# First expert unit of a hybrid encoder block: gather over four PSUM banks, expert order ahead of the weights, refills in smaller pieces

## The chip, the cores and the metric

One core of one Trainium2 chip runs the whole program. The metric is device time in microseconds (us); it is the slowest core's time, and here there is one core. All data are float32. The time of the kernel before is the median of three runs.

## The reference, cut to what matters

One encoder layer over 256 tokens of width 1024: RMS norm, projection, two attention groups, output projection and residual, then a two-level mixture of experts, then a final norm. The change lies where the attention part ends and the experts begin.

```python
def hier_moe(x, w_group, b_group, w_expert, b_expert, w_gate, w_up, w_down):
    xt = x.reshape(-1, d)                       # 256 tokens x 1024
    gl = xt @ w_group + b_group                 # 4 groups, top 1
    el = (xt @ w_expert + b_expert)             # 4 x 8 experts, top 2 in the group
    ...                                         # combine: weights of the two experts of a token
    for gi in range(4):                         # every expert: 1024x512, 1024x512, 512x1024
        h = silu(xt @ w_gate[gi]) * (xt @ w_up[gi])
        y = y + (h * combine[:, gi]) @ w_down[gi]
    return y
```

Each of the 32 experts has 3 matrices of 2 MiB, 201 MB in all, and every one is read from HBM once, whichever tokens chose it.

## The kernel before, in words

**Ring.** The weights of the experts pass through a ring of 12 slots of 2 MiB in SBUF. One matrix fills one slot: 16 KB in each of 128 partitions, which is 8 chunks of the contraction (KC = 8) of 2 KB each for gate and up. SP (SyncE) issues all weight DMAs on one queue, in a fixed order, and waits before each until the slot has been read.

**Units.** The 32 experts are worked off in ten units of 2 or 4 experts (WAYS = 2, 2, 4, 4, 2, 2, 4, 4, 4, 4). Units 0 and 1 are the fixed experts 0 to 3, so their 12 matrices are loaded during the attention part and fill the ring. From unit 2 on the experts are taken in order of how many tokens chose them. That order is known only after the router: it stands in `expert_at`, which VectorE (DVE) writes at L1096 with `order_ready`. SP reads the expert's number from there (`order_of`, L367 to L369, a register load for each expert) before it can issue the first load of unit 2.

**Refill of the first slots.** The two gate slots of unit 0 are refilled with the gate matrices of the first two experts of unit 2, in pieces (`GATE_PIECES`, `load_chunks`, L380 to L398): chunks 0 and 1, 2 and 3, then 4 to 7, each when TensorE (PE) has multiplied those chunks for both experts (`gate_pieces` at L1540, `gate_done`). The two up slots follow in halves (`load_piece`, L399 to L405, `up_half`), then down slots and unit 1's slots in halves. From unit 3 on whole slots are loaded (L435 to L440).

**Gather.** A unit's tokens are gathered by PE: a selection matrix `pick` (made by DVE, `make_picks`, L1028) is multiplied with the rows h, chunk by chunk and over the two token tiles. For unit 0 the first four chunks go to bank GD0 (`gather_tile`, L1543), tile 0 ahead of tile 1, so that PE can begin when `pick_first` is there; chunks 4 and 5 go to GD1, and chunks 6 and 7 to the same bank after the gate products of chunks 0 to 3. ScalarE (ACT, `gathered_out`, L705) takes chunks 0 to 3 out of PSUM, and signals each; DVE (L1048) takes the rest in two pieces (`xg_mid`, `xg_dve`). `first_gate` (L1530) multiplies a chunk once it is out.

**Order by hand on each engine.** PE, from the router's end: three constant products of 448 columns (`multiply_constants`, L1399, their results are not used), ranks of the first choices, one constant product, ranks of the second choices (`ranked`), four small products for the counts (`counted`), one constant product, `gather_tile`, `gather_chunks(1, 0..2)`, the product that turns the experts' places into an order (`ordered`, L1558), `first_gate` of 0..4, the gather of chunks 6 and 7, `first_gate` of the rest, then up. DVE, from `ranked` on: `rank1` (L1025), `make_picks`, the weights of the chosen experts (L1075 to L1080), `weigh_picks`, then counts, keys, places (L1084 to L1090), `wide_hot` (L1091), `place_hot` (L1093, `places_ready`), `expert_at`, `gathered_out(0)`.

Unit 1's gathers, transposes and unit 0's down products follow on PE (L1584 on). Its loop waits at L1601 until all early pieces of unit 2 have landed.

Of the kernel before, what the change touches and what calls it, by code (L numbers as in the profile page):

```python
# [10 lines left out]
ALU = mybir.AluOpType  # L11
# [23 lines left out]
GATE_PIECES = ((0, 2), (2, 4), (4, 8))  # L35
# [76 lines left out]
def fill_at(u, m, a):  # L112
    return 3 * sum(WAYS[:u]) + ways(u) * m + a
# [5 lines left out]
def build_encoder(nc, x, x_cols, norm1_g, w_in, qn_g, kn_g, sink, rel_bias, gnorm_a, gnorm_b, w_o, norm2_g,  # L119
# [11 lines left out]
    with ExitStack() as ctx:  # L131
# [131 lines left out]
        COUNTS, PICKS0, RANKS, ORDER = Y0, UP, Y2, Y3  # L263

# [24 lines left out]
        first_ready, second_ready, pick_first = map(sem, ("first_ready", "second_ready", "pick_first"))  # L289
# [25 lines left out]
        def _(sp):  # L315
# [83 lines left out]
            for k in range(2):  # L399
                if k == 0:  # L400
                    sp.wait_ge(up_half, 1)
                else:
                    sp.wait_ge(up_done, 1)
                load_piece(2, 0, 2, k, 2)
                load_piece(2, 0, 3, k, 2)  # L405
# [14 lines left out]
            for k in range(2):  # L420
                if k == 0:
                    sp.wait_ge(up_half, 2)
                else:
                    sp.wait_ge(up_done, 2)
                load_piece(2, 2, 0, k, 2, up_refill_in)
                load_piece(2, 2, 1, k, 2, up_refill_in)
# [144 lines left out]
        def _(act):  # L571
# [201 lines left out]
        def _(dve):  # L773
# [274 lines left out]
            def gathered_out(i):  # L1048
                if i == 0:
                    for k, done in enumerate((xg_mid, xg_dve)):  # L1050
                        dve.wait_ge(gathered, k + 2)
                        dve.tensor_tensor(xgT[:, 4 + 2 * k:6 + 2 * k, :], ps[GD1][:, 256 * k:256 * k + 256].rearrange("p (c s) -> p c s", c=2),
                                          bcast(g2_rows[:, 4 + 2 * k:6 + 2 * k], 2, P), ALU.mult).then_inc(done, 1)
                else:
                    dve.wait_ge(gathered, 2 * i + 3)
                    dve.tensor_tensor(xgT[:, 4:8, :], ps[GD1][:].rearrange("p (c s) -> p c s", c=4), bcast(g2_rows[:, 4:8], 2, P),  # L1056
                                      ALU.mult).then_inc(xg_dve, 1)
# [20 lines left out]
            k_second = mark(dve.tensor_tensor(w_second, hot2, bcast(w2, 3, PER_GROUP), ALU.mult))  # L1078
            after(k_second)
            link(dve.tensor_tensor(weight.rearrange("p t (g e) -> p t g e", g=GROUPS), w_first, w_second, ALU.add))  # L1080
# [8 lines left out]
            link(dve.tensor_reduce(place[0:EXPERTS], key_above[0:EXPERTS], AX_X, ALU.add))  # L1089
            link(dve.tensor_scalar(wide_e[0:EXPERTS], place[0:EXPERTS], float(WIDE), float(HALF_CAP), ALU.is_le, ALU.mult))  # L1090
            dve.tensor_tensor(wide_hot[0:EXPERTS], ident[0:EXPERTS, 0:EXPERTS],  # L1091
                              wide_e[0:EXPERTS].broadcast_to([EXPERTS, EXPERTS]), ALU.mult)
            dve.tensor_tensor(place_hot[0:EXPERTS], iota1[0:EXPERTS, 0:EXPERTS],  # L1093
                              place[0:EXPERTS].broadcast_to([EXPERTS, EXPERTS]), ALU.is_equal).then_inc(places_ready, 1)
            dve.wait_ge(ordered, 1)
            dve.tensor_copy(expert_at[:], ps[ORDER][0:1, 128:128 + EXPERTS]).then_inc(order_ready, 1)  # L1096
            gathered_out(0)
            make_picks(rank1, 2, 2)
# [86 lines left out]
        def _(pe):  # L1185
# [213 lines left out]
            def multiply_constants(n, bank):  # L1399
                for _ in range(n):  # L1400
                    pe.matmul(ps[bank][:, 0:448], ident, cst[:, 0:448], start=True, stop=True)
# [11 lines left out]
            multiply_constants(1, GATE)  # L1413
# [8 lines left out]
            multiply_constants(1, GATE)  # L1422
# [119 lines left out]

            def gather_tile(t, c):  # L1543
                return pe.matmul(ps[GD0][:, c * P:(c + 1) * P], h_cols[:, t, c, :], pick[:, t, :],
                                 start=(t == 0 and c == 0), stop=(t == TT - 1 and c == 3))
# [12 lines left out]
            pe.matmul(ps[ORDER][0:1, 128:128 + EXPERTS], expert_col, place_hot[0:EXPERTS], start=True, stop=True).then_inc(ordered, 1)  # L1558
# [6 lines left out]
            products(0, 2, fill_at(0, 1, 0), UP, up_done, up_half, KC // 2)  # L1565
# [18 lines left out]
            for i in range(1, UNITS):  # L1584
# [15 lines left out]
                if i == 2:  # L1600
                    pe.wait_ge(first_pieces_in, 16 * 2 * PIECES)  # L1601
# [125 lines left out]
```

## Time and profile before

| | |
|---|---|
| runs | 554.76, 555.28, 555.88 us, median 555.28 |
| profiled execution | span 553.0 us from the first to the last instruction; its own time is not listed apart from the runs, and the median is 2.3 us above the span |
| busy | PE 447.3 us (81%), PE weight loads 191.3, DVE 108.5, ACT 80.0, POOL 28.4 |
| DMA | 217.68 MB, mean 394 GB/s; the SP queue (q1) 214.84 MB, 93.5% of 16 engines' span |
| mean granted PE clock | 0.911 of 2.4 GHz |

A window row gives for a stretch of time the busy time of each engine with the number of its instructions, the granted PE clock as a share of full speed, the mean busy share of the 16 DMA engines and what they moved in GB/s. A timeline row gives start, duration, engine, line, operation, output and input, and how many instructions were merged. A "q" behind an engine means its instruction queue, as SPq for the DMA issues of SP.

### The profile page before, as it was taken

To read this page: it belongs to the slowest core of one execution; us is meant where nothing else is said; L and a number is where in the kernel's file an instruction comes from. 1 tells how busy PE (TensorE), PEld (TensorE's weight loads), DVE (VectorE), ACT (ScalarE), POOL (GpSimd) and SP (SyncE) were. 2 spreads that over 40 slices of the span, in tenths; PEclk is the share of its full clock that TensorE was granted. 3 is DMA by queue.
4 is the path that set the end of the run, shared out by engine and by line. 5 is a ranking of instruction groups with operands and counts; after the bars stand their busy time and mean duration, and the time that the engine had idled before them with its cause. 6 is when DMAs were issued, how large, how long until landed. Compare 5 with 4: busy or idle time off the path is not lost.

```text
span 553.0 us, 6311 instructions
## 1 busy us (share of the span) xinstructions
PE 447.3 (81%) x2496; PEld 191.3 (35%) x2496; DVE 108.5 (20%) x346; ACT 80.0 (14%) x212; POOL 28.4 (5%) x61
## 2 busy tenths in 40 slices
PE   8999999999999977569999984962784384666794
PEld 3455554664353332133442521410232021311231
DVE  1028863261140310020210400400031000400012
ACT  1127663221110101000101001000100001000103
POOL 0242422100000000000000000000000000000000
PEclk9999999999999999699999988876877887977999
DMA  8989995969999999999999999999999999999992
GB/s 314 352 320 422 395 339 180 373 247 364 424 420 423 427 429 424 429 427 430 425 428 430 422 430 425 430 425 429 429 425 430 425 428 428 427 428 430 420 387 105
DMA packets 26798, 217.68 MB, mean 394 GB/s; under 512 B 5224, under 2 KB 7016, under 8 KB 13200
## 3 DMA queue, kind: packets, MB, share of 16 engines
q1 hardware_dynamic: 22400, 214.84, 93.5%
q10 hardware_dynamic: 4368, 2.42, 1.5%
q8 instruction: 21, 0.34, 0.2%
q14 instruction: 9, 0.07, 0.0%
HBM read 216.18 MB, written 1.06 MB: 393 GB/s over the span
## 4 chain that ended last, share of the span: by engine, by line
PE 47%; DMA 44%; SPq 6%; issue 1%; DVE 1%; ACT 0%; POOLq 0%; POOL 0%; DVEq 0%; ACTq 0%
DMA ring<-in_w_down_dram 28%; PE bank L1466 11%; PE bank L1486 9%; DMA ring<-in_w_gate_dram 8%; PE bank L1201 7%; DMA ring<-in_w_up_dram 6%; PE bank L1289 5%; SPq L446 5%; PE bank L1427 2%; PE bank L1243 2%; PE bank L1267 1%; PE bank L1255 1%; PE bank L1520 1%; PE bank L1538 1%; PE bank L1528 1%; DMA ring<-in_w_in_dram 1%
## 5 line engine op out<-in xcount | busy, mean ns | idle before, releaser
L1466 PE MATMUL bank<-ring,head 128*32 128x512 f32 (+1 forms) x992 | 155.0, 676 | 69.7 <-DMA ring<-in_w_gate_dram 37.9
L1466 PEld LDWEIGHTS bank<-ring,head 128*32 128x32 f32 (+1 forms) x992 | 44.4, 128 | 170.9 <-issue 170.7
L1486 PE MATMUL bank<-ring,region_q 128*32 128x512 f32 (+1 forms) x512 | 79.5, 664 | 25.3 <-DMA ring<-in_w_down_dram 24.4
L1072 DVE COPY region_q<-bank 128x256 f32<-128x256 f32 x10 | 4.2, 424 | 301.8 <-PE bank L1445 301.8
L1486 PEld LDWEIGHTS bank<-ring,region_q 128*32 128x32 f32 (+1 forms) x512 | 23.0, 127 | 74.1 <-issue 70.4
L722 ACT ACTIVATE head<-bank 128x512 f32<-128x512 f32 x20 | 11.1, 595 | 243.2 <-PE bank L1520 229.6
L1201 PE MATMUL bank<-ring,head 128*128 128x512 f32 x96 | 43.1, 597 | 1.3 <-DMA ring<-in_w_in_dram 1.3
L1427 PEld LDWEIGHTS bank<-region_q,h 128*128 128x128 f32 x304 | 35.7, 192 | 9.1 <-issue 9.1
L1427 PE MATMUL bank<-region_q,h 128*128 128x128 f32 x304 | 38.5, 279 | 0.0
L1520 PE MATMUL bank<-head,region_q 128*128 128x512 f32 x72 | 33.3, 605 | 1.2 <-ACT head L722 1.2
L1289 PE MATMUL bank<-ring 128*128 128x512 f32 x64 | 29.7, 600 | 0.0
L708 ACT ACTIVATE head<-bank,head 128x128 f32<-128x128 f32 x40 | 11.4, 368 | 124.0 <-PE bank L1427 119.1
L1201 PEld LDWEIGHTS bank<-ring,head 128*128 128x128 f32 x96 | 17.5, 190 | 23.4 <-issue 22.5
L568 POOL TENSOR_TENSOR stat<-stat 128x1 f32<-128x1 f32 x2 | 1.1, 548 | 438.4 <-DVE stat L1168 438.4
L1520 PEld LDWEIGHTS bank<-head,region_q 128*128 128x128 f32 x72 | 12.9, 190 | 21.6 <-issue 19.6
L1289 PEld LDWEIGHTS bank<-ring 128*128 128x128 f32 x64 | 11.3, 190 | 10.8 <-issue 10.8
L1033 DVE TENSOR_SCALAR region_q<-cst,sorted_rw,stat 128x32 f32<-128x32 f32 (+1 forms) x56 | 12.4, 297 | 0.0
L1043 DVE TENSOR_SCALAR region_q<-cst,sorted_rw 128x32 f32<-128x32 f32 (+1 forms) x56 | 12.4, 297 | 0.0
L1066 DVE TENSOR_TENSOR region_q<-region_q,bank 128x512 f32<-128x512 f32 x10 | 6.9, 687 | 17.0 <-PE bank L1466 17.0
L1061 DVE COPY region_q<-bank 128x512 f32<-128x512 f32 x10 | 6.9, 692 | 16.0 <-PE bank L1480 16.0
L1056 DVE TENSOR_TENSOR head<-bank,head 128x512 f32<-128x512 f32 x9 | 6.2, 692 | 17.1 <-PE bank L1427 17.1
L855 DVE SCALAR_TENSOR_TENSOR h<-bank,stat,h 128x512 f32<-128x512 f32 x8 | 6.0, 751 | 16.4 <-PE bank L1289 9.8
(194 smaller groups left out, 290.9 us busy)
## 6 DMA issues: line engine op xcount, KB each, us to landing
ring<-in_w_gate_dram SPq DMA_DIRECT2D x28, 2048.0 KB, 39.4
ring<-in_w_up_dram SPq DMA_DIRECT2D x28, 2048.0 KB, 39.3
ring<-in_w_down_dram SPq DMA_DIRECT2D x24, 2048.0 KB, 38.1
ring<-in_w_down_dram SPq DMA_DIRECT2D x12, 1024.0 KB, 12.5
ring<-in_w_up_dram SPq DMA_DIRECT2D x8, 1024.0 KB, 10.6
ring<-in_w_gate_dram SPq DMA_DIRECT2D x6, 1024.0 KB, 9.4
ring<-in_w_o_dram SPq DMA_DIRECT2D x2, 2048.0 KB, 11.7
ring<-in_w_in_dram SPq DMA_DIRECT2D x7, 512.0 KB, 8.2
```

What stands on the lines that cost most here:

```text
L446: sp.dma_start(slots[fill_slot(fill_at(UNITS - 1, 2, a))][:, cols], down_e[bass.ds(experts[a], 1), :, cols].rearrange("a p d -> (a p) d")) ...
L708: last = act.activation(xgT[:, c, :], ps[GD0][:, c * P:(c + 1) * P], ACT.Copy, scale=g2_rows[:, c:c + 1])
L722: act.activation(y_slots[:, 512 * half:512 * half + 512], ps[(GD0 if i else Y0) + half][:], ACT.Copy).then_inc(y_ready, 1)
L1033: last = dve.tensor_scalar(pick[:, t, rows * a:rows * (a + 1)], iota1[:, 0:rows], ranks[:, t, e0 + a:e0 + a + 1], rstd2[:, t:t + 1], ALU.i ...
L1043: last = dve.tensor_scalar(pick_w[:, t, rows * a:rows * (a + 1)], iota1[:, 0:rows], ranks[:, t, e0 + a:e0 + a + 1], weights[:, t, e0 + a:e ...
L1201: return pe.matmul(ps[bank][:], xT[:, c, t * P:(t + 1) * P], cols, start=(c == 0), stop=(c == KC - 1))
L1243: last = pe.matmul(ps[2 * (s % 2) + half][:, 256 * j:256 * j + 256], qkT[rows, 5 * g + 2 * jg + j, qt * P:(qt + 1) * P], qkT[rows, 5 * g + ...
L1289: last = pe.matmul(ps[bank][:], mixT[:, 1 - g, t, c, :], w_o_sb[g][:, c, 512 * half:512 * half + 512], start=(c == 0), stop=(c == 3))
L1427: last = pe.matmul(ps[GD0 + b][:, c * P:(c + 1) * P], h_cols[:, t, 4 * b + c, :], pick[:, t, :], start=(t == 0), stop=(t == TT - 1))
L1466: last = pe.matmul(ps[bank][rows, :], xgT[:, c, rows], slots[fill_slot(f + a)][:, c * F:(c + 1) * F], start=(c == 0), stop=(c == KC - 1))
L1486: last = pe.matmul(ps[bank + half][rows, :], hT[:, c, rows], slots[fill_slot(f + a)][:, c * D + 512 * half:c * D + 512 * half + 512], star ...
L1520: last = pe.matmul(ps[Y0 + k][:], place_w[i % 2][:, (k // 2) * P:(k // 2 + 1) * P], y_slots[:, 512 * (k % 2):512 * (k % 2) + 512], start=( ...
```

## The change

Six edits, all around unit 0:

1. The gate refill of unit 2's first two experts goes in four pieces of two chunks instead of three pieces, the refill of the two up slots in quarters instead of halves (`up_half` now counts three times for unit 0).
2. The gather of unit 0 is written in four steps of two chunks (both token tiles), each into a bank of its own (GD0, Y1, GD1, Y2). The first two come first, the other two after the gate products of chunks 0 to 3. `pick_first` is gone: the gather waits for all of `pick`.
3. ACT waits for the first two chunks, then for the next two. DVE waits for steps 3 and 4.
4. On DVE the counts' keys, the places and `place_hot` come straight after `make_picks`; the weights, `wide_hot`, `counts` and `weigh_picks` come later.
5. PE makes the order's product right after the first two gather steps.
6. The constant product between the two ranks is 128 columns wide instead of 448; the one behind the counts is gone.

```diff
-GATE_PIECES = ((0, 2), (2, 4), (4, 8))
+GATE_PIECES = ((0, 2), (2, 4), (4, 6), (6, 8))
+        FIRST_BANKS = (GD0, Y1, GD1, Y2)
...
@@ SP
-            for k in range(2):
-                if k == 0:
-                    sp.wait_ge(up_half, 1)
+            for k in range(4):
+                if k < 3:
+                    sp.wait_ge(up_half, k + 1)
                 else:
                     sp.wait_ge(up_done, 1)
-                load_piece(2, 0, 2, k, 2)
-                load_piece(2, 0, 3, k, 2)
+                load_piece(2, 0, 2, k, 4)
+                load_piece(2, 0, 3, k, 4)
...
-                    sp.wait_ge(up_half, 2)
+                    sp.wait_ge(up_half, 4)
@@ ACT
-                act.wait_ge(gathered, 2 * i + (2 if i else 1))
+                if i:
+                    act.wait_ge(gathered, 2 * i + 3)
                 for c in range(4):
-                    last = act.activation(xgT[:, c, :], ps[GD0][:, c * P:(c + 1) * P], ACT.Copy, scale=g2_rows[:, c:c + 1])
+                    if i == 0 and c % 2 == 0:
+                        act.wait_ge(gathered, c // 2 + 1)
+                    last = act.activation(xgT[:, c, :], ps[GD0 if i else FIRST_BANKS[c // 2]][:, c * P:(c + 1) * P], ACT.Copy, scale=g2_rows[:, c:c + 1])
@@ DVE
-            make_picks(rank1, 0, 2, (pick_first, pick_ready))
-            k_w = mark(dve.tensor_tensor(w2, w1, e2, ALU.mult))
-            k_first = mark(dve.tensor_tensor(w_first, hot1_here, bcast(w1, 3, PER_GROUP), ALU.mult))
-            after(k_w)
-            k_second = ...
-            after(k_second)
-            link(... weight ...)
-            weigh_picks(rank1, weight, 0, 2)
-
+            make_picks(rank1, 0, 2, (None, pick_ready))
             dve.wait_ge(counted, 1)
-            dve.tensor_copy(counts, ps[COUNTS][:, 0:32])
             dve.tensor_tensor(key_row ...)
             link(... key_col ...)
             link(... key_above ...)
             link(dve.tensor_reduce(place ...))
+            dve.tensor_tensor(place_hot ...).then_inc(places_ready, 1)
+            k_w = ...
+            k_first = ...
+            dve.wait_ge(ordered, 1)
+            dve.tensor_copy(expert_at[:], ps[ORDER][0:1, 128:128 + EXPERTS]).then_inc(order_ready, 1)
             link(... wide_e ...)
-            dve.tensor_tensor(wide_hot ...)
-            dve.tensor_tensor(place_hot ...).then_inc(places_ready, 1)
-            dve.wait_ge(ordered, 1)
-            dve.tensor_copy(expert_at ...).then_inc(order_ready, 1)
+            dve.tensor_tensor(wide_hot ...).then_inc(order_ready, 1)
+            dve.tensor_copy(counts, ps[COUNTS][:, 0:32])
+            after(k_w)
+            k_second = ...
+            after(k_second)
+            link(... weight ...)
             gathered_out(0)
+            weigh_picks(rank1, weight, 0, 2)
@@ PE
-            multiply_constants(1, GATE)
+            multiply_constants(1, GATE, P)
...
-            multiply_constants(1, GATE)
...
-                    if c in (1, 3, KC - 1):
+                    if c in (1, 3, 5, KC - 1):
...
-            pe.wait_ge(pick_first, 1)
-            for c in range(4):
-                gather_tile(0, c)
+            def first_gather(k):
+                for c in (2 * k, 2 * k + 1):
+                    for t in range(TT):
+                        last = pe.matmul(ps[FIRST_BANKS[k]][:, c % 4 * P:(c % 4 + 1) * P], h_cols[:, t, c, :], pick[:, t, :],
+                                         start=(t == 0), stop=(t == TT - 1))
+                last.then_inc(gathered, 1)
+
             pe.wait_ge(pick_ready, 1)
-            for c in range(4):
-                last = gather_tile(1, c)
-            last.then_inc(gathered, 1)
-            gather_chunks(1, range(0, 2)).then_inc(gathered, 1)
-            for a in range(2):
-                landed(fill_at(0, 0, a))
-            pe.wait_ge(places_ready, 1)
-            pe.matmul(ps[ORDER] ...).then_inc(ordered, 1)
-            first_gate(range(0, 4))
-            pe.wait_ge(xg_mid, 1)
-            gather_chunks(1, range(2, 4)).then_inc(gathered, 1)
+            first_gather(0)
+            first_gather(1)
+            pe.wait_ge(places_ready, 1)
+            pe.matmul(ps[ORDER] ...).then_inc(ordered, 1)
+            for a in range(2):
+                landed(fill_at(0, 0, a))
+            first_gate(range(0, 4))
+            first_gather(2)
+            first_gather(3)
+            pe.wait_ge(xg_mid, 1)
             first_gate(range(4, 6))
             pe.wait_ge(xg_dve, 1)
             first_gate(range(6, KC))
-            products(0, 2, fill_at(0, 1, 0), UP, up_done, up_half, KC // 2)
+            products(0, 2, fill_at(0, 1, 0), UP, up_done, up_half)
...
-                pe.wait_ge(order_ready, 1)
+                pe.wait_ge(order_ready, 2)
...
-                    pe.wait_ge(first_pieces_in, 16 * 2 * PIECES)
+                    pe.wait_ge(first_pieces_in, 16 * 2 * (PIECES + 2))
```

## Rows read from the trace of the kernel before

**Rows 1.** The page, part 2: GB/s in 40 equal slices of 13.8 us.

```profile
GB/s 314 352 320 422 395 339 180 373 247 364 424 420 423 427 429 424 429 427 430 425 428 430 422 430 425 430 425 429 429 425 430 425 428 428 427 428 430 420 387 105
```

**Rows 2.** The chain that ended last: shares by engine, and its last wait.

```profile
PE 47%; DMA 44%; SPq 6%; issue 1%; DVE 1%; ACT 0%; POOLq 0%; POOL 0%; DVEq 0%; ACTq 0%
...
522.20 17.91 DMA ring<-in_w_down_dram
```

**Rows 3.** Windows: us, five engines' busy times, clock, DMA share, GB/s.

```profile
117.40:121.20 3.80, 3.78 (x26) 2.22 (x26) 1.77 (x12) 2.42 (x5) 0.00 (x0) 1.00 0.03 6
121.20:122.20 1.00, 1.00 (x8) 0.29 (x4) 0.00 (x0) 0.00 (x0) 0.00 (x0) 1.00 0.00 0
122.20:129.50 7.30, 7.30 (x40) 3.00 (x38) 1.32 (x5) 0.60 (x1) 0.00 (x0) 1.00 0.90 277
129.50:141.26 11.76, 11.76 (x70) 5.91 (x68) 1.38 (x2) 1.14 (x4) 0.00 (x0) 1.00 1.00 405
141.26:181.90 40.64, 39.77 (x239) 17.04 (x236) 9.17 (x33) 3.52 (x8) 0.00 (x0) 1.00 1.01 422
181.90:500.00 318.10, 229.83 (x1418) 89.17 (x1417) 37.25 (x124) 19.01 (x49) 0.00 (x0) 0.86 1.01 428
```

**Rows 4.** What SP's DMA queue waited for, 117 to 129 us.

```profile
SPq L369 <- DVE expert_at L1096: 12.7, 1, 12.7
```

**Rows 5.** Timeline and line view of SP's DMA issues.

```profile
121.22 0.36 SPq L384 DMA_DIRECT2D ring<-in_w_gate_dram  x1
...
122.35 1.42 SPq L384 DMA_DIRECT2D ring<-in_w_gate_dram  x3
...
127.61 0.34 SPq L384 DMA_DIRECT2D ring<-in_w_gate_dram  x1
...
141.26 4.24 SPq L376 DMA_DIRECT2D ring<-in_w_up_dram  x4
...
L340 SPq DMA_DIRECT2D ring<-in_w_gate_dram x4: 332/332/342, 181.9 to 183.5; - x4
```

**Rows 6.** Timeline of PE, DVE and ACT, 113 to 124 us.

```profile
113.28 1.00 PE L1401 MATMUL bank<-cst 128*128 128x448 f32 x2
...
114.78 0.22 DVE L1025 SCALAR_TENSOR_TENSOR rank<-bank,region_q 128x64 f32<-128x64 f32 x1
...
115.03 0.98 DVE L1033 TENSOR_SCALAR region_q<-cst,rank,stat 128x64 f32<-128x64 f32 x4
...
115.23 1.02 PE L1401 MATMUL bank<-cst 128*128 128x448 f32 x2
...
116.09 1.95 PE L1544 MATMUL bank<-region_q,h 128*128 128x128 f32 x16
...
117.66 0.17 DVE L1085 TENSOR_TENSOR region_q<-bank,cst 32x32 f32<-32x32 f32 x1
...
118.08 1.14 ACT L708 ACTIVATE head<-bank,head 128x128 f32<-128x128 f32 x4 [4.86 <-PE bank L1544]
...
118.34 0.14 DVE L1090 TENSOR_SCALAR region_q<-region_q 32x1 f32<-32x1 f32 x1
...
118.63 0.17 DVE L1093 TENSOR_TENSOR stat<-cst,region_q 32x32 f32<-32x32 f32 x1
...
118.95 0.21 PE L1558 MATMUL bank<-stat,cst 32*1 32x32 f32 x2
119.09 3.65 PE L1538 MATMUL bank<-ring,head 128*64 128x512 f32 x16
119.20 0.18 DVE L1096 CAST expert_at<-bank 1x32 int32<-1x32 f32 x1 [0.40 <-PE bank L1558]
...
122.67 1.16 PE L1427 MATMUL bank<-region_q,h 128*128 128x128 f32 x8
```

**Rows 7.** Windows as in rows 3: small packets, and a gap on PE.

```profile
128.00:129.00 1.00, 1.00 (x8) 0.32 (x6) 0.00 (x0) 0.06 (x1) 0.00 (x0) 1.00 1.03 410
531.00:535.00 4.00, 4.00 (x40) 2.77 (x36) 1.38 (x2) 1.19 (x2) 0.00 (x0) 1.00 1.02 399
166.50:167.70 1.20, 0.33 (x5) 0.17 (x5) 0.69 (x1) 0.00 (x0) 0.00 (x0) 1.00 1.03 430
```

More of the change, by code:

```diff
@@ L288, in build_encoder @@
         gexp_asked, e2_asked, chosen_ready, ranked, counted, flag_ready = map(sem, ("gexp_asked", "e2_asked", "chosen_ready", "ranked", "counted", "flag_ready"))
-        first_ready, second_ready, pick_first = map(sem, ("first_ready", "second_ready", "pick_first"))
+        first_ready, second_ready = map(sem, ("first_ready", "second_ready"))
         k_squared, ssk_ready, final_g_turned, final_g_cut = map(sem, ("k_squared", "ssk_ready", "final_g_turned", "final_g_cut"))
@@ L1050, in gathered_out @@
                     for k, done in enumerate((xg_mid, xg_dve)):
-                        dve.wait_ge(gathered, k + 2)
-                        dve.tensor_tensor(xgT[:, 4 + 2 * k:6 + 2 * k, :], ps[GD1][:, 256 * k:256 * k + 256].rearrange("p (c s) -> p c s", c=2),
+                        dve.wait_ge(gathered, k + 3)
+                        dve.tensor_tensor(xgT[:, 4 + 2 * k:6 + 2 * k, :], ps[FIRST_BANKS[2 + k]][:, 256 * k:256 * k + 256].rearrange("p (c s) -> p c s", c=2),
                                           bcast(g2_rows[:, 4 + 2 * k:6 + 2 * k], 2, P), ALU.mult).then_inc(done, 1)
                 else:
-                    dve.wait_ge(gathered, 2 * i + 3)
+                    dve.wait_ge(gathered, 2 * i + 4)
                     dve.tensor_tensor(xgT[:, 4:8, :], ps[GD1][:].rearrange("p (c s) -> p c s", c=4), bcast(g2_rows[:, 4:8], 2, P),
@@ L1089, in _ @@
             link(dve.tensor_reduce(place[0:EXPERTS], key_above[0:EXPERTS], AX_X, ALU.add))
+            dve.tensor_tensor(place_hot[0:EXPERTS], iota1[0:EXPERTS, 0:EXPERTS],
+                              place[0:EXPERTS].broadcast_to([EXPERTS, EXPERTS]), ALU.is_equal).then_inc(places_ready, 1)
+            k_w = mark(dve.tensor_tensor(w2, w1, e2, ALU.mult))
+            k_first = mark(dve.tensor_tensor(w_first, hot1_here, bcast(w1, 3, PER_GROUP), ALU.mult))
+            dve.wait_ge(ordered, 1)
+            dve.tensor_copy(expert_at[:], ps[ORDER][0:1, 128:128 + EXPERTS]).then_inc(order_ready, 1)
             link(dve.tensor_scalar(wide_e[0:EXPERTS], place[0:EXPERTS], float(WIDE), float(HALF_CAP), ALU.is_le, ALU.mult))
             dve.tensor_tensor(wide_hot[0:EXPERTS], ident[0:EXPERTS, 0:EXPERTS],
-                              wide_e[0:EXPERTS].broadcast_to([EXPERTS, EXPERTS]), ALU.mult)
-            dve.tensor_tensor(place_hot[0:EXPERTS], iota1[0:EXPERTS, 0:EXPERTS],
-                              place[0:EXPERTS].broadcast_to([EXPERTS, EXPERTS]), ALU.is_equal).then_inc(places_ready, 1)
-            dve.wait_ge(ordered, 1)
-            dve.tensor_copy(expert_at[:], ps[ORDER][0:1, 128:128 + EXPERTS]).then_inc(order_ready, 1)
+                              wide_e[0:EXPERTS].broadcast_to([EXPERTS, EXPERTS]), ALU.mult).then_inc(order_ready, 1)
+            dve.tensor_copy(counts, ps[COUNTS][:, 0:32])
+            after(k_w)
+            k_second = mark(dve.tensor_tensor(w_second, hot2, bcast(w2, 3, PER_GROUP), ALU.mult))
+            after(k_second)
+            link(dve.tensor_tensor(weight.rearrange("p t (g e) -> p t g e", g=GROUPS), w_first, w_second, ALU.add))
             gathered_out(0)
+            weigh_picks(rank1, weight, 0, 2)
             make_picks(rank1, 2, 2)
@@ L1397, in _, with multiply_constants @@
             router_logits(1, range(4, 8)).then_inc(routed, 1)
-            def multiply_constants(n, bank):
+            def multiply_constants(n, bank, cols=448):
                 for _ in range(n):
-                    pe.matmul(ps[bank][:, 0:448], ident, cst[:, 0:448], start=True, stop=True)
+                    pe.matmul(ps[bank][:, 0:cols], ident, cst[:, 0:cols], start=True, stop=True)
             def rank_tiles(hot, start):
@@ L1539, in first_gate @@
                                          start=(c == 0), stop=(c == KC - 1))
-                    if c in (1, 3, KC - 1):
+                    if c in (1, 3, 5, KC - 1):
                         last.then_inc(gate_done if c == KC - 1 else gate_pieces, 1)
-            def gather_tile(t, c):
-                return pe.matmul(ps[GD0][:, c * P:(c + 1) * P], h_cols[:, t, c, :], pick[:, t, :],
-                                 start=(t == 0 and c == 0), stop=(t == TT - 1 and c == 3))
-            pe.wait_ge(pick_first, 1)
-            for c in range(4):
-                gather_tile(0, c)
+            def first_gather(k):
[4 more added lines that the diff above has]
+                last.then_inc(gathered, 1)
             pe.wait_ge(pick_ready, 1)
-            for c in range(4):
-                last = gather_tile(1, c)
-            last.then_inc(gathered, 1)
-            gather_chunks(1, range(0, 2)).then_inc(gathered, 1)
+            first_gather(0)
+            first_gather(1)
+            pe.wait_ge(places_ready, 1)
+            pe.matmul(ps[ORDER][0:1, 128:128 + EXPERTS], expert_col, place_hot[0:EXPERTS], start=True, stop=True).then_inc(ordered, 1)
             for a in range(2):
                 landed(fill_at(0, 0, a))
-            pe.wait_ge(places_ready, 1)
-            pe.matmul(ps[ORDER][0:1, 128:128 + EXPERTS], expert_col, place_hot[0:EXPERTS], start=True, stop=True).then_inc(ordered, 1)
             first_gate(range(0, 4))
+            first_gather(2)
+            first_gather(3)
             pe.wait_ge(xg_mid, 1)
-            gather_chunks(1, range(2, 4)).then_inc(gathered, 1)
             first_gate(range(4, 6))
```

2 lines of the change are left out of this document (removed).

## The prediction, made blind

> **What bounds the kernel now.** I read the slices of the page first. GB/s stands at 420 to 430 from the eleventh slice to the last but two, and in the seventh to tenth it is 180, 373, 247 and 364 [rows 1]. So this is a kernel that streams 217 MB, and it loses time where the stream stops. The chain that ended last says the same: DMA 44%, and PE 47% in the part before the stream takes over. Its last wait is a DMA of a down matrix from 522.20 for 17.91 us, and from there a tail of 12.9 us runs to the end of the span at 553.0 [rows 2]. The windows show where the stream stops: from 117.40 to 121.20 nothing but a remnant moves (6 GB/s), from 122.20 to 129.50 it comes up at 277, then 405, then 422 up to 181.90 and 428 from there to 500 [rows 3]. From 181.90 on the engine busy shares do not matter. Every microsecond by which the stream starts earlier after 117.4 moves the end by as much, if the stream does not stop again.
>
> Who starts it? SP's queue waited 12.7 us for `expert_at` [rows 4]. The order was written at 119.20 + 0.18 = 119.38, but the first issue is at 121.22, the second at 122.35 (a register load for the next expert lies between) and two more follow within 1.42 us [rows 5]. The first gate products run from 119.09 for 3.65 us, four chunks [rows 6], so chunks 0 and 1 are done about 1.8 to 1.9 us after their start, at 121.0. The later of SP's two conditions is thus PE having read the slots, not the order. A stream that starts earlier needs the gate products earlier.
>
> **The change part by part.**
>
> *Constant product between the ranks, 448 to 128 columns.* Two passes take 1.00 us from 113.28 [rows 6]; the second choices are ready in their midst. 320 columns less in each pass, at 1.00 us for two passes of 448 with their fixed parts, can free at most 0.5 us of PE. But the four rank products behind keep their own load-and-multiply chain, and DVE reaches `rank1` only after its own weights' arithmetic. `rank1` starts at 114.78 [rows 6]. Bounds are 0 and 0.2 us; I take 0.13.
>
> *The constant product behind the counts goes.* It takes 1.02 us from 115.23, and the gather starts at 116.09 behind it [rows 6]. The new gather waits for all of `pick`. The picks run from 115.03 to 116.01; with 0.13 off, 115.88, plus about 0.25 us from DVE's signal to PE's first product (weights must be loaded first): 116.13. So the gather starts where it did, and the constants' 1.02 us is worth nothing here: it was hidden behind the picks. In exchange PE stands for some 0.7 us. In a like gap, 166.50 to 167.70 with PE busy 0.33, the granted clock stayed 1.00 [rows 7]. I cost it at nothing; if the clock fell to 1.2 GHz, the gather and gate products would stretch, and this step with them.
>
> *Gather in four steps.* 16 instructions take 1.95 us and the 8 of chunks 4 and 5 another 0.9, up to 118.9; only then come the order's product (118.95) and the first gate product (119.09) [rows 6]. Now steps 0 and 1 are 16 instructions and step 2 and 3 come later: the order's product can run at 116.13 + 1.95 = 118.08 and the gate products at 118.10, if their inputs are there. ACT needs 1.14 us for four chunks [rows 6], some 0.37 for the first one, and now starts on chunk 0 after half of the gather, at 117.2; it has chunk 0 at 117.6, chunk 3 at 118.8. No stall. Gate products start 1.0 us earlier.
>
> *Order ahead of weights.* From the first key at 117.66 to `place_hot` at 118.63 + 0.17 are 1.14 us, and `wide_e` at 118.34 shows where `place_hot` can now stand: 0.29 earlier [rows 6]. Right behind the picks that gives 115.85 + 0.68 + 0.17 = 116.7, two microseconds before 118.8. PE is not there to use it until 118.1, so the order is written at about 118.35, 1.0 us earlier. SP needs less than the 1.13 us between its first two issues to turn it into an address [rows 5], so it is ready by 119.5 and then waits for the gate chunks, as now. The weights and `weigh_picks` come later on DVE; they are first needed by unit 1, more than 10 us on, so nothing waits.
>
> *First refill.* Chunks 0 and 1 are read 1.0 us earlier: 118.10 + 1.9 = 120.0; issue at 120.2 instead of 121.22. The second expert's load stays 1.13 us behind it, pieces 3 and 4 come at 121.9 and 122.4. **Gain of the stream's start: 1.0 us** (bounds 0.3, if ACT or the places are late, and 1.2).
>
> *PE afterwards.* Steps 2 and 3 (16 instructions, about 2.0 us) take the place of one piece of 8 in 1.16 us at 122.67 [rows 6]. So PE gives back 0.85 of its 1.0 us: gate ends about 0.1 us earlier than now, and so do up and all that follows. `xg_mid` comes one multiply on DVE after step 2; step 3 (0.9 us) covers it.
>
> *Finer refills.* Twelve issues of 512 KB take the place of six of 1 MB, at about 0.43 us of SP each, every 1.7 us or so: SP has time. They come earlier only for chunks 4 and 5 (about 125.7 instead of 127.61) and quarters 1 and 3. Is the stream short of work there now? From 122.20 to 141.26 it moved 277 x 7.30 + 405 x 11.76 = 6.8 MB, and four matrices, 8.4 MB, had been issued: 1.6 MB, 3.8 us, were still queued at the 141.26 issue [rows 3, 5]. The same sum at 181.90 gives 23.9 of 25.2 MB, 2.9 us queued; less the 1.0 us from the issue at 121.22 to the first bytes after 122.20 [rows 3, 5], 1.9 us of slack. Two things follow: earlier issues find the queue full already, so they gain little; and a stream moved ahead by 1.0 us against PE's 0.1 does not run dry at either place, but nothing over 2.0 us could be gained in this way.
>
> What do they cost? Packets halve to 4 KB. The nearest rows: 410 GB/s in 128 to 129, when 4 KB pieces alone move from a filled queue; 399 in 531 to 535, with 4 and 2 KB packets [rows 7]; and 277 in the opening [rows 3]. The same 6.3 MB moved at about 405 in 8 KB packets, 15.5 us. At 410 they cost nothing or bring 0.2 us, at 399 they cost 0.25, at 277 they would take 22.7 us, 7.2 more. The queue is filled, so I stay near 399 and take **0.3 us lost**.
>
> **Sum.** 1.0 - 0.3 = 0.7 us off the span of 553.0, so 552.3, and with the 2.3 us that lie around the profiled span to the median of the runs, 554.6. That is 0.13% of 555.28; a measurement of this kernel tells about 0.2%, 1.1 us, from no change.
>
> **The rivals.**
>
> *A, small pieces starve the stream (slower).* Place: 128 to 144 us, the twelve pieces. The opening shows what 512 KB pieces do when each meets a short queue: 2.0 MB in 7.3 us [rows 3]. Whatever first bytes cost would be paid twelve times. It decides below 6.3 MB in 16.5 us, 381 GB/s: there the 1.0 us is gone. At 350 the stretch takes 18.0 us and the kernel 555.28 + 2.5 - 1.0 = 556.8; at 277 it would be 561.5. Against it: 3.8 us are queued. The Trainium skill, DMA: Bandwidth & Descriptors, section Bandwidth, has the rule "Batch DMAs to ≥1 MiB for ≥75% of peak", with 341 GB/s for a single 1 MB; by that figure, an estimate, the stretch would take 18.4 us and the kernel come to 557.2. The trace speaks against the rule for a queue with work in it, with 410 GB/s in 512 KB pieces. Chance 0.12.
>
> *B, the finer pieces feed the opening (larger gain).* The opening lost 7.3 - 2.0/0.423 = 2.5 us and the stretch behind it another 0.5. If that comes of few packets in flight, pieces 5 and 6, now 2 us earlier, and the quarters win back about 1 us. Up to the cap of 2.0: 553.3. For it: 405 against 422 with the queue not dry. Against it: the slow part is pieces 1 to 3, whose spacing the change leaves alone. Chance 0.25.
>
> *C, the start does not move.* One of the inputs is late (ACT's chunks, or the gather behind `pick_ready` instead of `pick_first`), and the first issue stays at about 121: 555.5 with the small packets' price. Chance 0.10.
>
> **How the numbers follow.** Forecast 0.53, A 0.12, B 0.25, C 0.10. The likeliest is 554.6, its own range 553.9 to 555.3 by the bounds of start and packets. Half a microsecond more for the scatter of the runs (554.76 to 555.88) puts some 0.1 of the forecast's chance over the 1.1 us mark; with most of B that is 0.34 faster. Same is the rest of the forecast with C and the near part of A, 0.54; slower 0.12. The range, 553.2 to 556.6, takes in B, C and A down to 355 GB/s.
>
> **What the profile after would show.** Right: the order written at 118.3 to 118.5, the first gate product at 118.1, the first gate refill issued at 120.1 to 120.4, gate products ending within 0.2 us of 127.4, no slow window between 129 and 182, the last down transfer landing 0.5 to 1 us earlier. Wrong start: an issue after 120.6. Wrong packets: under 395 GB/s from 130 to 144. Wrong cap: a window under 400 GB/s behind 141 or 182. A PE clock of 0.5 near 116 would overthrow the PE part.

## The result and the profile after

The changed kernel came out slower: 556.18 us median of 19 runs against 555.18 of the kernel before, ratio 1.0027, 95% interval 1.0016 to 1.0037, so 1.5 us (0.9 to 2.1) by the ratio; the two medians differ by 1.0. The forecast was 0.7 us faster. In a later comparison (e11 below) the same kernel stood at 0.9998 (0.9979 to 1.0017). Why one kernel gives both is the subject of what follows, and part of it stays open.

The page of the changed kernel, its span, its slices and its chain:

```profile
span 554.0 us, 6326 instructions
...
PEclk9999999989999999689999998977978887977898
...
GB/s 313 350 323 426 388 337 188 366 247 353 419 421 421 425 428 429 426 429 430 421 431 427 428 425 429 426 429 428 426 431 426 425 429 427 428 427 431 418 385 99
...
PE 47%; DMA 43%; SPq 7%; DVE 1%; issue 1%; ACT 0%; POOLq 0%; POOL 0%; DVEq 0%; ACTq 0%
```

Against [rows 1] the stream is no better where it was to gain: 247 in the ninth slice as before, 353 for 364 in the tenth. And PEclk has an 8 in the ninth slice, 111 to 125 us. Windows of the changed kernel (columns as in [rows 3]) show that place, and then the stretches of [rows 3]:

```profile
114.90:115.77 0.87, 0.00 (x1) 0.00 (x1) 0.87 (x6) 0.00 (x0) 0.00 (x0) 1.00 1.10 471
...
116.80:120.20 3.40, 3.40 (x16) 2.16 (x16) 0.88 (x6) 2.13 (x5) 0.00 (x0) 0.50 0.20 80
...
122.20:129.50 7.30, 7.30 (x44) 3.51 (x42) 2.63 (x10) 0.60 (x1) 0.00 (x0) 1.00 0.87 291
...
129.50:141.26 11.76, 11.76 (x70) 5.88 (x68) 1.38 (x2) 1.14 (x4) 0.00 (x0) 1.00 1.00 381
141.26:181.90 40.64, 39.76 (x236) 17.07 (x236) 9.17 (x33) 3.52 (x8) 0.00 (x0) 1.00 1.01 420
181.90:500.00 318.10, 229.16 (x1430) 89.38 (x1422) 37.33 (x124) 19.02 (x49) 0.00 (x0) 0.88 1.01 427
```

PE stood for 0.87 us behind the counts, and from 116.80 to 120.20 its granted clock was 0.50, the 1.2 GHz level. Behind that the stream moved at 381 where it had moved at 405. From 141 on the two kernels are alike. The timeline of the changed kernel shows what the half clock did:

```profile
110.45 0.26 DVE L970 SCALAR_TENSOR_TENSOR region_q<-bank,stat,router_b 128x36 f32<-128x36 f32 x1 [1.16 <-PE bank L1385]
...
114.47 0.22 DVE L1029 SCALAR_TENSOR_TENSOR rank<-bank,region_q 128x64 f32<-128x64 f32 x1
...
115.77 2.88 PE L1548 MATMUL bank<-region_q,h 128*128 128x128 f32 x16 [0.87 <-DVE region_q L1037]
...
116.32 0.18 DVE L1085 TENSOR_TENSOR stat<-cst,region_q 32x32 f32<-32x32 f32 x1
...
118.76 4.35 PE L1540 MATMUL bank<-ring,head 128*64 128x512 f32 x16
118.87 0.18 DVE L1090 CAST expert_at<-bank 1x32 int32<-1x32 f32 x1 [2.16 <-PE bank L1556]
...
121.59 2.55 SPq L385 DMA_DIRECT2D ring<-in_w_gate_dram  x4
```

The 16 gather instructions took 2.88 us for 1.95 in [rows 6], the 16 of the gate 4.35 for 3.65. `place_hot` (L1085) was there at 116.50 (forecast 116.7), two microseconds before PE could use it. But the order was written at 119.05, and the first refill issued at 121.59, not 120.2: 0.37 us later than before, where 1.0 us earlier was wanted.

**How the profiles are compared.** The attention part ahead of all this ends at another time in each execution: the router's last logits, the DVE row at 110.45 above, came between 109.7 and 112.4 us over all profiles. So each is read from its own such row, called R. The row of the kernel before, for R = 110.57:

```profile
110.57 0.25 DVE L966 SCALAR_TENSOR_TENSOR region_q<-bank,stat,router_b 128x36 f32<-128x36 f32 x1 [1.16 <-PE bank L1382]
```

The first issue then stands at R + 10.65 before and at R + 11.14 after. And the refill wave is measured by what the DMA engines moved from R + 9 to R + 36, a window of 27 us: 1 GB/s more or less there is 27/423 = 0.064 us of the stream that follows at 423. Six profiles of the changed order with small pieces and an undisturbed clock will give 337 to 343, so one profile is good to some 3 GB/s, 0.2 us. Windows of the kernel before and the changed one:

```profile
119.57:146.57 27.00, 27.00 (x144) 11.95 (x142) 3.53 (x9) 3.88 (x8) 0.00 (x0) 1.00 0.88 336
```

```profile
119.45:146.45 27.00, 27.00 (x145) 12.21 (x142) 4.34 (x14) 3.98 (x8) 0.00 (x0) 0.99 0.87 325
```

11 GB/s less, 0.7 us lost by R + 36. In the 40 us behind it the two move 423 and 421 GB/s, 0.2 us more, and that is no more than such windows scatter (421 to 423 over all kernels).

### The profile page after: what moved, and what is told of

It is laid out like the page before. It is cut to its first block, busy times and chain, and to the rows that moved or that the text cites. A ratio compares the mean times of both kernels' runs of the same rounds, so it can differ in the third digit from the quotient of the medians.

```text
span 554.0 us, 6326 instructions
## 1 busy us (share of the span) xinstructions
PE 446.0 (81%) x2494; PEld 191.4 (35%) x2494; DVE 108.4 (20%) x346; ACT 80.2 (14%) x212; POOL 28.7 (5%) x61
## 4 chain that ended last, share of the span: by engine, by line
PE 47%; DMA 43%; SPq 7%; DVE 1%; issue 1%; ACT 0%; POOLq 0%; POOL 0%; DVEq 0%; ACTq 0%
DMA ring<-in_w_down_dram 28%; PE bank L1468 11%; PE bank L1488 9%; DMA ring<-in_w_gate_dram 8%; PE bank L1204 7%; DMA ring<-in_w_up_dram 6%; SPq L447 6%; PE bank L1292 5%; PE bank L1429 2%; PE bank L1246 2%; PE bank L1270 1%; PE bank L1258 1%; PE bank L1540 1%; PE bank L1522 1%; PE bank L1530 1%; DMA ring<-in_w_in_dram 1%
## 5 line engine op out<-in xcount | busy, mean ns | idle before, releaser
L726 ACT ACTIVATE head<-bank 128x512 f32<-128x512 f32 x20 | 11.1, 595 | 240.4 <-PE bank L1522 225.7
L1429 PEld LDWEIGHTS bank<-region_q,h 128*128 128x128 f32 x288 | 33.7, 192 | 8.2 <-issue 8.2
L1429 PE MATMUL bank<-region_q,h 128*128 128x128 f32 x288 | 36.3, 279 | 0.0
```

Of the source, the lines that this page charges most:

```text
L726: act.activation(y_slots[:, 512 * half:512 * half + 512], ps[(GD0 if i else Y0) + half][:], ACT.Copy).then_inc(y_ready, 1)
L1429: last = pe.matmul(ps[GD0 + b][:, c * P:(c + 1) * P], h_cols[:, t, 4 * b + c, :], pick[:, t, :], start=(t == 0), stop=(t == TT - 1))
```

## The experiments

**First: are there two losses, and do they add?** Edits against the changed kernel (e1, e2, e3) and against the kernel before (e4).

e1, the constant product back behind the counts:

```diff
             pe.matmul(ps[COUNTS][0:EXPERTS, 32:33], chosen[:, 1, :], ones[:, 0:1], start=False, stop=True).then_inc(counted, 1)
+            multiply_constants(1, GATE)
```

> The changed kernel with the constant product of 448 columns behind the counts put back, nothing else. Clock theory (PE idle for 0.87 us behind the counts let the granted clock fall to 0.5 from 116.8 to 120.2, and that ate the earlier start): the clock stays at 1.00, the first gate product starts at 118.1, the first gate refill is issued at 120.2 instead of 121.6, and the time is 1.4 us below the changed kernel, 0.1 us above the kernel before. Packet theory alone (the twelve 512 KB pieces cost all of the loss): the time stays 1.5 us above the kernel before, though the first issue moves. Rival (the PE gap has nothing to do with the clock): the clock still falls at 116.8 and the issue stays at 121.6.

e2, the old piece sizes, no constant product:

```diff
-GATE_PIECES = ((0, 2), (2, 4), (4, 6), (6, 8))
+GATE_PIECES = ((0, 2), (2, 4), (4, 8))
...
-            for k in range(4):
+            for k in range(2):
...
-                load_piece(2, 0, 2, k, 4)
-                load_piece(2, 0, 3, k, 4)
+                load_piece(2, 0, 2, k, 2)
+                load_piece(2, 0, 3, k, 2)
```

with the semaphores' counts as before the change.

> The changed kernel with the refills in the old sizes (gate in three pieces, up in halves), nothing else; no constant product behind the counts, so the clock fall should stay. Packet theory: 129.5 to 144 moves at 405 GB/s or more instead of 381, mean landing of the last up piece 0.9 us earlier, time 0.9 us below the changed kernel, 0.6 above the kernel before. Clock theory alone: no difference to the changed kernel, 1.5 us above the kernel before.

e3, both edits:

> The changed kernel with both put back: the constant product behind the counts and the old piece sizes. What is left is the gather in four steps, the order ahead of the weights and the narrow product between the ranks. If the two losses add (1.4 and 0.9 us): 2.3 us below the changed kernel, 0.8 us below the kernel before, first issue at 120.2, clock 1.00 throughout. If something else in the new order costs time: no better than the kernel before.

e4, the kernel before with the pieces of the change, e2's edit the other way round:

> The kernel before with the finer refills alone (gate in four pieces, up in quarters). Packet theory: 0.9 us above the kernel before, with 381 GB/s in 129.5 to 141.3 against 405. If the finer pieces cost only where the clock fall delays PE: 0 to 0.2 us.

Measured against the kernel before on the same chip (interval in brackets; the row "changed" is from the first comparison):

| | first issue, us after R | GB/s, R+9 to R+36 | clock near the gather | ratio |
|---|---|---|---|---|
| before | 10.65 | 336 | 1.00 | |
| changed | 11.14 | 325 | 0.50 | 1.0027 (1.0016 to 1.0037) |
| e1 filler | 9.57 | 337 | 1.00 | 1.0002 (0.9984 to 1.0020) |
| e2 coarse | 9.57 | 349 | 1.00 | 1.0019 (0.9998 to 1.0039) |
| e3 both | 9.57 | 351 | 1.00 | 0.9996 (0.9975 to 1.0016) |
| e4 before, fine | 10.66 | 333 | 1.00 | 1.0006 (0.9988 to 1.0024) |

The windows of e1 to e4 in this order, each from its own kernel:

```profile
120.88:147.88 27.00, 27.00 (x148) 12.55 (x146) 4.70 (x13) 3.26 (x8) 0.00 (x0) 1.00 0.92 337
```

```profile
119.29:146.29 27.00, 27.00 (x148) 12.55 (x146) 4.70 (x13) 3.27 (x8) 0.00 (x0) 1.00 0.91 349
```

```profile
118.98:145.98 27.00, 27.00 (x148) 12.54 (x146) 4.70 (x13) 3.26 (x8) 0.00 (x0) 1.00 0.91 351
```

```profile
119.07:146.07 27.00, 27.00 (x144) 11.94 (x142) 3.53 (x9) 3.90 (x8) 0.00 (x0) 1.00 0.89 333
```

e1 and e3 had the first issue where the forecast had put it, 1.1 us earlier than before. Between e1 and e3 lie only the piece sizes: 14 GB/s, 0.9 us. In the kernel before the same pieces took 3 GB/s, 0.2 us, which is within the scatter of one profile. The times of whole runs are too wide to tell these four apart. e1's time was where clock theory had it. e3's was 0.2 us below the kernel before and not 0.8, with an interval that holds both. The surprise was e2: no constant product, the same gap on PE (0.86 us), and no fall of the clock. The clock theory as I had put it, gap means fall, had failed.

**Second: is the fall a matter of chance, and what else is to be gained?** e8 is e2 once more; e5 puts a constant product of 128 columns where e1 has 448; e6 has old piece sizes and takes out all constant products there. e7 is e3 with one edit on SP:

```diff
-            experts = order_of(2, range(1))
+            experts = order_of(2, range(2))
...
-                if k == 0:
-                    experts += order_of(2, range(1, 2))
```

> The kernel of e2 once more (changed kernel, old piece sizes, no constant product behind the counts). In e2's profile the clock had not fallen, in the changed kernel's it had, with the same work on PE up to there. Chance theory (with this gap the clock falls in some executions and not in others): either is possible; if it falls, the first issue stands at 11.1 us after the router's last logits instead of 9.6, and the last transfer of the first refill wave about 1.2 us later than in e2. Rival (the piece sizes decide over the clock): it does not fall here either. Time over all runs 0.5 to 1 us above the kernel before.

> The changed kernel with old piece sizes and a constant product of 128 columns behind the counts instead of 448: PE's gap shrinks from 0.87 to about 0.6 us. Chance theory: the clock falls less often than without it; in one profile either can show. If it stays, first issue at 9.6 us after the router's last logits; if it falls, at about 11.1.

> The changed kernel with old piece sizes and no constant products at all between the router and the gather (the three, the one between the ranks, the one behind the counts all gone): PE stands for most of the 5 us. Clock theory: the clock falls in every execution, and earlier; the first gate product and the first issue come 1.4 to 2.5 us later than in e3, relative to the router's last logits (issue at 11 to 12 us instead of 9.6). Rival (gaps do not matter to the clock here): issue at 9.6 or earlier, clock 1.00.

> The kernel of e3 (constant product behind the counts back, old piece sizes) with SP reading the numbers of both first experts before its first issue, where it waits for the gate chunks anyway; so the second expert's piece follows the first by 0.5 us instead of 1.13. Opening theory (the stream comes up slowly because its second piece comes late): mean landing of the fourth piece 0.5 us earlier after the router's last logits than in e3 (17.6 instead of 18.1 us), time 0.5 us below e3, about 1.3 us below the kernel before. Rival (the opening is slow by itself, whatever is queued): no difference to e3.

In e8 the clock fell, with the same code as e2. Its gap, its half clock and its refill wave (R = 111.44):

```profile
115.89:116.75 0.86, 0.00 (x1) 0.00 (x1) 0.86 (x6) 0.00 (x0) 0.00 (x0) 1.00 1.02 438
117.58:120.99 3.41, 3.41 (x17) 2.46 (x18) 0.99 (x7) 1.76 (x5) 0.00 (x0) 0.50 0.20 79
...
120.44:147.44 27.00, 27.00 (x145) 12.21 (x142) 4.51 (x16) 4.15 (x9) 0.00 (x0) 0.99 0.84 324
```

324 GB/s against e2's 349: **one fall of the clock costs 25 GB/s, 1.6 us, of one and the same kernel.** The first issue came at R + 11.13, as in the changed kernel and 1.56 us later than in e2, so the later start is the whole price. e8's ten runs lie between 551.96 and 557.47, four of them at or under 553.11 and six from 554.49 up; e8's ratio is 0.9992 (0.9971 to 1.0012). Two kinds of executions could look like that. But R alone scatters by 2.7 us over the profiles, and the runs without a profile show neither their R nor their clock there.

e5: a gap of 0.45 us, no fall, first issue at R + 9.58, 345 GB/s; one profile settles nothing. In e6 PE stood from 110.47 for 2.35 us, and the clock fell 2.1 us after the gap's start, before its end, and for twice as long:

```profile
110.47:112.82 2.35, 0.00 (x1) 0.00 (x0) 2.21 (x16) 0.21 (x1) 0.00 (x0) 0.94 1.03 439
112.60:119.40 6.80, 6.27 (x30) 6.12 (x31) 3.98 (x26) 0.83 (x3) 0.00 (x0) 0.50 0.73 312
```

First issue at R + 11.41, 315 GB/s in its refill wave.

e7 had the fourth piece landed at R + 17.44 against e3's 18.14 (mean of the 16 engines' landings). Over all undisturbed profiles of the new order the fourth piece landed at R + 17.76 to R + 18.42 with the number read between the pieces (ten profiles, mean 18.08), and at 17.44 to 17.72 with it read early (e7, e9, e12, mean 17.59): the opening did gain 0.5 us, as expected. But by R + 36 e7 stood where e3 stood, at 349 GB/s against 351. The hole is behind the fourth piece, for the next one is a whole half slot and waits for the end of the gate products:

```profile
128.00:130.00 2.00, 2.00 (x12) 0.70 (x10) 0.00 (x0) 0.00 (x0) 0.00 (x0) 1.00 0.90 229
```

e7's runs gave 0.9983 (0.9970 to 0.9997), the first kernel to beat the kernel before beyond its interval.

**Third: which of the finer pieces costs?** e9 is e7 and e10 is e3, each with the gate refill in four pieces as in the change and the up refill still in halves:

```diff
-GATE_PIECES = ((0, 2), (2, 4), (4, 8))
+GATE_PIECES = ((0, 2), (2, 4), (4, 6), (6, 8))
...
-                    if c in (1, 3, KC - 1):
+                    if c in (1, 3, 5, KC - 1):
```

> The kernel of e7 with the gate refill in four pieces as in the changed kernel, the up refill still in halves. In e7 the stream had a hole: 229 GB/s from 128 to 130, because the fourth piece was in before the next, whole-half piece could be issued. Feeding theory: the hole closes (over 350 GB/s there), the last up piece lands 0.9 to 1.4 us earlier after the router's last logits than in e7 (34.05), capped by what unit 2's last slots allow (1.2 us), time 0.9 us below e7, about 1.9 below the kernel before. Packet theory (every 512 KB piece costs by its size): no difference to e7 or 0.2 us worse.

> The kernel of e3 with the gate refill in four pieces, the up refill in halves, no early reading of the second number. With e1 (all fine) and e3 (all coarse) it tells which half of the finer refills costs. Feeding theory: p4 to last up piece 15.92 us in e3, 16.93 in e1; here 15.0 to 15.4, as the hole of e3 (315 GB/s from 128 to 130) closes and the up pieces stay large; time 0.6 us below e3. Packet theory: 16.3, halfway between e1 and e3, time 0.4 above e3.

e9 and e10, R + 9 to R + 36:

```profile
119.75:146.75 27.00, 27.00 (x148) 12.55 (x146) 4.70 (x13) 3.26 (x8) 0.00 (x0) 1.00 0.93 349
```

```profile
119.43:146.43 27.00, 27.00 (x148) 12.54 (x146) 4.70 (x13) 3.26 (x8) 0.00 (x0) 1.00 0.92 338
```

e9 closed the hole (356 GB/s from 128 to 130) and won nothing by R + 36, 349 as e7. e10 fell to 338 from e3's 351, with four small pieces in place of two larger ones. From the fourth piece to the last up piece it took 16.5 us, against the 15.0 to 15.4 of the feeding theory. The packet theory had said 16.3, but e5 and e7, with the old sizes, took 16.6 as well, so this length does not speak for it. The feeding theory, my rival B, thus falls in both as to its net gain, and no single price per piece fits both either; why is not shown. Ratios: e9 0.9975 (0.9957 to 0.9994), e10 0.9973 (0.9953 to 0.9993). e7, e9 and e10 all beat the kernel before; among themselves they cannot be told apart. e10's ratio is 1.5 us (0.4 to 2.6) below the kernel before where its profile puts it only 2 GB/s, 0.1 us, ahead: the times of whole runs hold something of this size that these windows do not show.

**Fourth: the changed kernel again, and how often its clock falls.** e11 is the changed kernel and e12 is e7, unaltered and together. e13, e14 and e15 are one profile each of the changed kernel, and e16 takes the narrow product between the ranks out of it:

```diff
-            multiply_constants(1, GATE, P)
             pe.wait_ge(second_ready, 1)
```

> The changed kernel once more, unaltered, on the same chip as e12. If the clock falls in this profile too, the first issue stands at 11.1 us after the router's last logits, if not at 9.6. Time by both theories together (clock falls in most executions, twelve small pieces cost 0.4 to 0.9 us): 0.5 to 1.5 us above the kernel before.

> The kernel of e7 once more, on the same chip as e11: clock 1.00 to 200 us, first issue at 9.6 us after the router's last logits, last transfer of the first refill wave at 34.05; time 0.9 us below the kernel before (ratio 0.998) and 1.5 to 2.5 us below the changed kernel.

> The changed kernel, one profile. If the clock falls: first issue 11.1 us after the router's last logits, last gate and up refill wave landed 1.1 us later than in e11. If not: 9.6, as in e11. Phase theory (whether the gap makes the clock fall depends on when it comes): about half of the looks fall. Rival (e11 and e2 were odd): all fall.

> The same once more: either 11.1 us with a clock of 0.5 around the gather, or 9.6 with 1.00; no third value of the first issue.

> The same once more: either 11.1 us with a clock of 0.5 around the gather, or 9.6 with 1.00; no third value of the first issue.

> The changed kernel without the narrow constant product between the ranks too, so that PE stands a little more, in two places. Phase theory: either is possible, fall more likely than without the edit. If this gap decided alone it would fall. First issue 9.6 without a fall, 10.5 to 11.4 with one.

| | first issue, us after R | GB/s, R+9 to R+36 | clock | time, ratio |
|---|---|---|---|---|
| e11 changed | 9.57 | 340 | 1.00 | 0.9998 (0.9979 to 1.0017) |
| e12 = e7 | 9.56 | 352 | 1.00 | 0.9968 (0.9948 to 0.9988) |
| e13 changed | 9.58 | 343 | 1.00 | 553.97 us, one run |
| e14 changed | 9.57 | 341 | 1.00 | 556.38 us, one run |
| e15 changed | 9.58 | 337 | 1.00 | 554.51 us, one run |
| e16 no narrow | 9.57 | 337 | 1.00 | 554.19 us, one run |

The same gap, and the wave of the changed kernel without a fall, from e11 (R = 110.50):

```profile
114.95:115.82 0.87, 0.01 (x1) 0.01 (x1) 0.87 (x6) 0.00 (x0) 0.00 (x0) 1.00 1.23 527
...
119.50:146.50 27.00, 27.00 (x148) 12.54 (x146) 4.70 (x13) 3.26 (x8) 0.00 (x0) 1.00 0.93 340
```

e11's time, expected 0.5 to 1.5 us above the kernel before, was 0.1 us below it (1.0 below to 0.9 above). So of five profiles of the changed kernel one shows the fall; of all eight with this gap (these, e2, e8, e16) two. With the 448 columns behind the counts none of eight does (before, e1, e3, e4, e7, e9, e10, e12). Two falls among sixteen profiles would both land in one given half about one time in four by luck, so that the filler keeps the clock up is likely, and not shown by these counts; e6, with a longer gap and an earlier, longer fall, speaks for it. In the eight with the gap of 0.87 us the first issues came at R + 9.6 or R + 11.1 and nowhere between. e14's 556.38 us with no fall is no contradiction: its R was 112.44, and the attention part had taken 2 us more ahead of the change.

In the comparison of e12 with e11 on the same chip the medians are 553.16 and 554.70 us: 1.5 us for the filler, the old sizes and the earlier reading, as expected there. The two profiles show half of it: 352 against 340 GB/s are 0.8 us.

## Why the prediction was wrong

**The start of the stream: right.** Every step of that sum was found where no clock fell. First issue 1.1 us earlier (forecast 1.0), the places 1.3 us ahead of their use (forecast 1.4; e11, `place_hot` done at 116.54, used at 117.80), no stall on ACT, the gather at the same R + 5.3 with the constants' 1.02 us (e3) and without them (e11). The gate products ended 0.2 us earlier than before (forecast 0.1; R + 16.66 in e11, R + 16.84 before).

**"I cost it at nothing": the step that failed.** I took PE's gap of 0.7 us (it is 0.87) to be harmless because a like gap at 166.50 had left the clock at 1.00 [rows 7], and named the fall only as a thing that would overthrow the step. In the profile of the changed kernel it did: the clock stood at 0.50 for 3.4 us, and the first issue came 0.5 us later than before where it comes 1.1 us earlier without a fall. One fall costs 1.6 us (e8 against e2). One row with a like gap was no bound. The same gap left the clock alone in six profiles and halved it in two. What decides between them is not shown; it is not the time since the program's start, for the gap began at 114.90 where the clock fell and at 114.95 in e11, where it did not. Three of the prediction's signs of being wrong came in that profile: an issue after 120.6 (121.59), under 395 GB/s from 130 to 144 (386), and the clock of 0.5 near 116.

**The finer refills: mis-sized.** Forecast 0.3 us lost. Without a fall the changed order moved 337 to 343 GB/s with them (e1, e11, e13 to e16) and 345 to 352 without (e2, e3, e5, e7, e12), on average 339 and 349: 10 GB/s, 0.6 us. With them the gain at the start is nearly used up: 340 against 336 before leaves 0.3 us, hardly more than the scatter of one profile. Two stretches, R + 9 to R + 19 and R + 19 to R + 36, show that the pieces gain first and lose more afterwards. e11 with the small pieces:

```profile
119.50:129.50 10.00, 10.00 (x54) 4.36 (x52) 2.63 (x10) 0.93 (x2) 0.00 (x0) 1.00 0.79 261
129.50:146.50 17.00, 17.00 (x96) 8.19 (x94) 2.07 (x3) 2.33 (x6) 0.00 (x0) 1.00 1.01 386
```

and e3 with the old ones:

```profile
118.98:128.98 10.00, 10.00 (x54) 4.36 (x52) 2.63 (x10) 0.93 (x2) 0.00 (x0) 1.00 0.74 236
128.98:145.98 17.00, 17.00 (x96) 8.18 (x94) 2.07 (x3) 2.33 (x6) 0.00 (x0) 1.00 1.01 419
```

The first brings 25 GB/s over 10 us, 0.6 us; the second loses 33 over 17 us, 1.3 us. On average over the profiles named above it is 0.4 us won and 1.0 us lost. The DMA share is 1.01 in both second rows, and the seven 512 KB gate pieces that e11 issued from 129.5 to 146.5 took 9.5 us at the median to land, e3's 1 MB ones 9.4, so the queue was as long and the engines as busy: what differed is the rate. I had costed 4 KB packets at 399 to 410 GB/s from a row of 1 us and one of 4 us, and they moved at 386 to 400 over 17 us. In the kernel before the same pieces cost 0.2 us (e4, 406 against 413 in the 17 us); why less there is not shown. With a fall they cost nothing on top (325 fine, 324 coarse, one profile each). So the two losses do not add, as e3's expectation had them.

**A term that the sum left out.** I put the same 2.3 us around the span on both sides. Over their runs the kernel before (and e4) takes 1.8 us more than its span, and the changed kernel and its variants 2.0 to 2.1. So 0.2 us are lost outside the span; what takes them is not shown.

**Rival A** had the right place and sign, and largely its price there. In its place, 128 to 144 us or R + 17.4 to R + 33.4, the kernel before moved 407 GB/s and the changed order with small pieces and without a fall 370 to 394 (e1, e11, e13 to e16, on average 379), about its break-even of 381; what it had not in its sum is the 0.4 us that the opening wins. That the changed kernel's row for 129.5 to 141 also says 381 is chance, for there the clock had fallen. The 341 GB/s that it took from the Trainium skill, DMA: Bandwidth & Descriptors, section Bandwidth, were too dark, for no profile went under 370 there. **Rival B** was right that the finer pieces feed the opening, and its net gain fell in e9 and e10. **Rival C** did not come.

**What stays open.** The profiles put the changed kernel 0.3 us ahead of the kernel before without a fall and 0.7 to 0.9 behind with one, 0.1 ahead and 0.9 to 1.1 behind with the 0.2 us outside the span. The span less R, another reading of the same profiles, says much the same: 442.4 us before, 442.0 to 442.6 for the changed kernel without a fall, 443.6 with it. One fall in five would make the two equal within 0.2 us, which is what e11's ratio of 0.9998 says. The first comparison's 1.5 us (0.9 to 2.1) would need a fall in most or all of its executions. Whether the fall was so much commoner there, or an attention part that happened to take longer (R went from 109.7 to 112.4 in five profiles of the changed kernel alone), or something else that no profile shows, is not settled: runs without a profile tell neither R nor their clock at that place.

## What to carry to other kernels

Products on constants are not idle work: before one is removed, look what would then stand on PE, and take several profiles of the result: the same code with a gap of under 1 us had its clock halved in one profile and not in the next, and one execution shows one outcome only. A shift of a stage is worth what is left at the next one: here 0.3 of 1.1 us survived behind smaller pieces. Split a refill only where the queue is seen to run dry, and check the piece behind the hole, too; in e7 and e9 the same bytes were there by R + 36 with and without it.

## What the runs showed that I had not expected

The clock at 0.50 for 3.4 us after a gap of 0.87 us, with PE busy throughout between the gap and the fall and all through the fall; and for 6.8 us in e6. The fall began 1.9 us after the gap's start in the changed kernel and 1.7 us in e8, when PE had been at work again for 1.0 and 0.8 us, so it does not answer the gap itself at once. And a stream that comes up from empty is slow for long: in the ten microseconds from its first packet, 1.0 us behind the first issue, it delivered 284 to 321 GB/s over all kernels. The kernel before, then e5, among the slowest, and e9, the fastest:

```profile
122.20:132.20 10.00, 10.00 (x52) 3.90 (x50) 1.32 (x5) 0.60 (x1) 0.00 (x0) 1.00 0.92 304
```

```profile
121.18:131.18 10.00, 10.00 (x56) 4.50 (x54) 2.63 (x10) 0.60 (x1) 0.00 (x0) 1.00 0.85 284
```

```profile
121.29:131.29 10.00, 10.00 (x56) 4.50 (x54) 2.63 (x10) 0.60 (x1) 0.00 (x0) 1.00 0.96 321
```

The earlier second piece of e7 moved the fourth piece's landing by 0.5 us and the total at R + 36 by nothing.
